# Two query blocks of the forgetting heads share a bank, a mask product and a place of transposes

## The reference

```python
def block(args):
    i, qd, qf, cq = args
    ...
    sf = jnp.einsum('bqhd,bkhd->bhqk', qf, fk).astype(jnp.float32) * (FOX_HEAD_DIM ** -0.5)
    sf = sf + jnp.transpose(cq, (0, 2, 1))[..., :, None] - cum_k[..., None, :]
    pf = jax.nn.softmax(jnp.where(causal, sf, NEG), axis=-1)
    of = jnp.einsum('bhqk,bkhd->bqhd', pf.astype(fv.dtype), fv)
```

## Time and profile before

| | us |
|---|---|
| median of 3 runs | 1096.33 (1096.22 to 1096.59) |
| span of the profiled execution | 1095.5 |
| PE busy in it | 1082.5 |
| ACT busy | 569.1 |
| DVE busy | 539.3 |
| POOL busy | 433.3 |

### The profile page before, as it was taken

How to read it: one execution, slowest core, us unless ns; L and a number is a source line. 1 busy time by engine, 2 the same in 40 slices (tenths; PEclk the granted TensorE clock), 3 DMA queues, 4 the chain that set the end, 5 groups by cost and what they waited for, 6 DMA issues and landing times.

```text
span 1095.5 us, 14926 instructions
## 1 busy us (share of the span) xinstructions
PE 1082.5 (99%) x5685; PEld 888.8 (81%) x5685; DVE 539.3 (49%) x1155; ACT 569.1 (52%) x1086; POOL 433.3 (40%) x236
## 2 busy tenths in 40 slices
PE   8999999999999999999999999999999999999998
PEld 7878878778887788888778787789888888888886
DVE  3739789788765224142445455535111115544444
ACT  6556767777678642353565565555222224333333
POOL 4234342342433344553143322344444445444441
PEclk9999999999999999999999999999999999999999
DMA  8133121221322332623222321222333333322312
GB/s 254 52 97 87 40 77 40 78 59 39 97 59 58 96 96 96 230 78 81 78 70 66 97 78 58 77 80 79 112 96 96 96 97 127 104 97 96 97 58 77
DMA packets 140530, 97.24 MB, mean 89 GB/s; under 512 B 9014, under 2 KB 125091, under 8 KB 140459
## 3 DMA queue, kind: packets, MB, share of 16 engines
q1 hardware_dynamic: 138728, 95.03, 29.4%
q10 hardware_dynamic: 1730, 1.25, 0.4%
HBM read 94.14 MB, written 2.91 MB: 89 GB/s over the span
## 4 chain that ended last, share of the span: by engine, by line
PE 95%; ACT 2%; DVE 1%; DMA 1%; issue 0%; POOL 0%; SPq 0%; ACTq 0%; DVEq 0%
PE bank L467 32%; PE bank L1196 14%; PE bank L1214 14%; PE bank L508 4%; PE bank L893 4%; PE bank L867 4%; PE bank L877 4%; PE bank L1227 2%; PE bank L686 1%; PE bank L617 1%; PE bank L629 1%; PE bank L710 1%; PE bank L1042 1%; PE bank L1004 1%; PE bank L482 1%; PE bank L1024 1%
## 5 line engine op out<-in xcount | busy, mean ns | idle before, releaser
L2485 POOL TENSOR_TENSOR ring<-raw_ring,ring 128x1024 fp32r<-128x1024 f32 x160 | 386.8, 2421 | 569.3 <-ACT ring L1241 569.3
L467 PE MATMUL bank<-hT,ring 128*128 128x512 f32 x1536 | 394.9, 402 | 0.7 <-ACT rawsb L1316 0.5
L467 PEld LDWEIGHTS bank<-hT,ring 128*128 128x128 f32 x1536 | 277.9, 188 | 57.9 <-issue 6.5
L1241 ACT CAST ring<-raw_ring 128x1024 fp32r<-128x1024 f32 x160 | 167.3, 1047 | 109.6 <-PE bank L1214 88.8
L1196 PE MATMUL bank<-hT,ring 128*128 128x512 f32 x672 | 152.5, 389 | 0.0
L1214 PE MATMUL bank<-ring,ring_u 128*128 128x512 f32 x672 | 152.5, 389 | 0.0
L1214 PEld LDWEIGHTS bank<-ring,ring_u 128*128 128x128 f32 x672 | 126.2, 188 | 26.2
L1196 PEld LDWEIGHTS bank<-hT,ring 128*128 128x128 f32 x672 | 126.1, 188 | 26.1
L2460 DVE TENSOR_TENSOR ring_u<-u,ring_u 128x1024 fp32r<-128x1024 f32 x32 | 80.7, 2529 | 73.8 <-ACT ring_u L1821 73.8
L2465 DVE TENSOR_TENSOR u<-u 128x512 f32<-128x512 f32 x32 | 22.9, 714 | 138.8 <-ACT u L1828 138.8
L1828 ACT ACTIVATE u<-bank 128x512 f32<-128x512 f32 x32 | 19.1, 598 | 114.9 <-PE bank L1196 108.4
(11 more groups left out here) (296 smaller groups left out, 1493.3 us busy)
## 6 DMA issues: line engine op xcount, KB each, us to landing
raw_ring<-in_w_in SPq DMA_DIRECT2D x144, 256.0 KB, 3.3
raw_ring<-in_w_up SPq DMA_DIRECT2D x64, 256.0 KB, 3.2
raw_ring<-in_w_down SPq DMA_DIRECT2D x64, 256.0 KB, 2.8
raw_ring<-in_w_out SPq DMA_DIRECT2D x32, 256.0 KB, 2.9
x<-in_x SPq DMA_DIRECT2D x8, 512.0 KB, 5.4
raw_ring<-in_w_branch_sb SPq DMA_DIRECT2D x8, 256.0 KB, 2.7
raw_ring<-in_w_branch_gdn SPq DMA_DIRECT2D x8, 256.0 KB, 3.2
cum<-cums SPq DMA_DIRECT2D x4, 512.0 KB, 5.5
```

The source lines that it names most:

```text
L467: p = pe.matmul(bank, m.slab_k8(n % 4)[:, a, k, :], m.hT[:, b, k, :], start=term == 0, stop=term == 23)
L1241: act.copy(m.ring[:, q, 0, :], m.raw_ring[:, q, :]).then_inc(s.slab_hi[q], 1)
L2485: pool.tensor_tensor(m.ring[:, q, 1, :], m.raw_ring[:, q, :], m.ring[:, q, 0, :].bitcast(F32), ALU.subtract).then_inc(s.slab_lo[q], 1)
```

## The change

The blocks of a forgetting head are handled in three units instead of four steps: unit 0 holds blocks 0 and 1 (128 and 256 columns side by side in the bank), unit 1 is block 2, unit 2 is block 3. For unit 0 there are still two maxima, two exponentials, two scalings and two copies per head, but one negation, one reciprocal and one mask product of 256 columns. `fox_z(i, 0)` issues twelve score matmuls at the place where it issued six, the separate place of block 1 is gone, and the six transposes of unit 0 stand together behind `diff_rows_T(i, 0, 0)`. On DVE and ACT the orders are set anew to match; semaphore counts change with them. In the last group the later places move too: block 2's scores stand at `tiles.to(41)`, block 3's ahead of `diff_z(i, 0, 1, 1)`, and on ACT and DVE block 3's exponentials and maxima stand ahead of the last `diff_exp` and `diff_weights`.

```diff
+FOX_UNITS = ((0, 1), (2,), (3,))
+FOX_STEPS = (0, 6, 10, 14)
+FOX_ACT = (0, 4, 6, 8)
+def fox_parts(u):
+    at = 0
+    for n, t_ in enumerate(FOX_UNITS[u]):
+        yield n, t_, at, at + (t_ + 1) * P
+        at += (t_ + 1) * P
 # TensorE
+    def fox_z(i, u):
...
         for k, (a, b) in enumerate(PARTS):
+            for n, t_, low, high in fox_parts(u):
+                for h in range(2):
+                    hp = slice(64 * h, 64 * h + 64)
+                    pe.matmul(banks[6 + h][:, low:high], qf[hp, a, t_ * P:(t_ + 1) * P], kf[hp, b, 0:high - low],
+                              start=k == 0 and n == 0, stop=k == 2, skip_group_check=n > 0)
         for h in range(2):
+            if u == 0:
+                o = banks[6 + h].rearrange("p (n w) -> p n w", n=2)[:, :, 0:P]
+                mask = m.causal_b.unsqueeze(1).broadcast_to([P, 2, P])
...
+            pe.matmul(o, m.ident_b, mask, start=False, stop=True, skip_group_check=True).then_inc(s.f_ps[h], 1)
 # TensorE, early groups
         fox_z(i, 0)
-        tiles.to(31)
-        fox_rows_T(i, 0, 0)
-        tiles.to(34)
-        fox_rows_T(i, 1, 0)
         tiles.to(51)
         diff_rows_T(i, 1, 0, pairs)
         tiles.to(54)
         diff_rows_T(i, 0, 0, pairs)
-        fox_z(i, 1)
+        fox_rows_T(i, 0, 0)
+        fox_rows_T(i, 1, 0)
         tiles.to(58)
         diff_av(i, 1, 0, pairs)
         tiles.to(63)
         diff_av(i, 0, 0, pairs)
-        fox_rows_T(i, 1, 1)
-        fox_rows_T(i, 0, 1)
 # TensorE, last group
-    tiles.to(20)
+    tiles.to(28)
+    diff_rows_T(i, 0, 0, last_pairs)
     fox_rows_T(i, 1, 0)
     fox_rows_T(i, 0, 0)
-    tiles.to(25)
-    tiles.to(28)
-    diff_rows_T(i, 0, 0, last_pairs)
-    fox_z(i, 1)
     tiles.to(41)
     diff_rows_T(i, 1, 0, last_pairs)
-    fox_rows_T(i, 1, 1)
+    fox_z(i, 1)
     tiles.to(46)
-    fox_rows_T(i, 0, 1)
     diff_av(i, 1, 0, last_pairs)
-    tiles.to(47)
     tiles.to(48)
     diff_z(i, 1, 1, 0, last_pairs)
-    fox_z(i, 2)
     diff_z(i, 1, 1, 1, last_pairs)
     tiles.to(49)
     diff_av(i, 0, 0, last_pairs)
+    fox_rows_T(i, 0, 1)
+    fox_rows_T(i, 1, 1)
     tiles.to(53)
     diff_z(i, 0, 1, 0, last_pairs)
-    fox_rows_T(i, 0, 2)
-    fox_rows_T(i, 1, 2)
+    fox_z(i, 2)
     diff_z(i, 0, 1, 1, last_pairs)
     tiles.to(54)
     diff_rows_T(i, 1, 1, last_pairs)
     tiles.to(55)
-    fox_z(i, 3)
     diff_rows_T(i, 0, 1, last_pairs)
...
 # ScalarE, early groups
         tile_b(g)
         diff_exp(i, 1, 0, 0)
-        fox_p(i, 0, 0)
         diff_exp(i, 0, 0, 0)
         diff_exp(i, 1, 0, 1)
         diff_exp(i, 0, 0, 1)
-        fox_p(i, 1, 0)
         diff_p(i, 0, 0, 2)
         diff_p(i, 1, 0, 4)
-        fox_exp(i, 0, 1)
-        fox_exp(i, 1, 1)
+        fox_p(i, 0, 0)
+        fox_p(i, 1, 0)
         tile_b(g + 1)
...
 # ScalarE, last group
     split(SLABS_OUT2 + 5)
-    fox_exp(i, 0, 2)
-    fox_exp(i, 1, 2)
+    fox_p(i, 0, 1)
+    fox_p(i, 1, 1)
     diff_square(i, 0, 0)
     diff_exp(i, 1, 1, 0)
     diff_exp(i, 1, 1, 1)
-    fox_p(i, 0, 2)
-    fox_p(i, 1, 2)
+    fox_exp(i, 0, 2)
+    fox_exp(i, 1, 2)
     diff_exp(i, 0, 1, 0)
     diff_exp(i, 0, 1, 1)
     diff_p(i, 1, 1, 5)
     diff_p(i, 0, 1, 4)
-    fox_exp(i, 0, 3)
-    fox_exp(i, 1, 3)
...
 # VectorE, early groups
         fox_max(i, 0, 0)
         fox_max(i, 1, 0)
+        diff_max(i, 1, 0, 1, 5)
+        diff_max(i, 0, 0, 0, 2)
+        diff_max(i, 0, 0, 1, 3)
         fox_recip(i, 0, 0)
-        diff_max(i, 1, 0, 1, 5)
         fox_normed(i, 0, 0)
         fox_recip(i, 1, 0)
         fox_normed(i, 1, 0)
-        diff_max(i, 0, 0, 0, 2)
-        diff_max(i, 0, 0, 1, 3)
         diff_weights(i, 1, 0)
         diff_weights(i, 0, 0)
...
 # VectorE, last group, from diff_weights(i, 1, 0) on, as it is after the change
+    fox_max(i, 0, 1)
+    fox_max(i, 1, 1)
+    diff_o(i, 1, 0, 5)
+    fox_recip(i, 0, 1)
+    fox_recip(i, 1, 1)
+    fox_normed(i, 0, 1)
+    fox_normed(i, 1, 1)
+    diff_max(i, 1, 1, 0, 5)
+    diff_max(i, 1, 1, 1, 5)
+    diff_o(i, 0, 0, 4)
+    diff_max(i, 0, 1, 0, 4)
+    diff_weights(i, 1, 1)
+    fox_max(i, 0, 2)
+    fox_max(i, 1, 2)
+    diff_max(i, 0, 1, 1, 4)
+    diff_weights(i, 0, 1)
+    fox_recip(i, 0, 2)
+    fox_normed(i, 0, 2)
+    fox_recip(i, 1, 2)
+    fox_normed(i, 1, 2)
+    diff_o(i, 1, 1, 5)
+    diff_o(i, 0, 1, 4)
```

More of the change, by code:

```diff
@@ L1700, in diff_mix, with fox_exp, fox_p @@
         act.copy(m.mix[:, 0, i, :], banks[bank]).then_inc(s.d_mhi, 1)
[L1702 to L1712, removed]
+    def fox_exp(i, h, u):
+        st = m.stat[:, 32 + 6 * h:38 + 6 * h]
+        act.wait_ge(s.f_dve[h], 14 * i + FOX_STEPS[u] + len(FOX_UNITS[u]) + 1)
+        for n, _, low, high in fox_parts(u):
+            sc = fox_rows[h][:, low:high]
+            act.activation(sc, sc, ACT.Exp, bias=st[:, n:n + 1], accum_out=st[:, 2 + n:3 + n]).then_inc(s.f_act[h], 1)
+    def fox_p(i, h, u):
+        act.wait_ge(s.f_ps[h], 7 * i + 2 * u + 2)
+        for _, t_, low, high in fox_parts(u):
+            dst = m.fox_wT[:, 3 - t_, 4 - t_:5, :] if h else m.fox_wT[:, t_, 0:t_ + 1, :]
+            act.copy(dst.rearrange("p c f -> p (c f)"), banks[6 + h][:, low:high]).then_inc(s.f_act[h], 1)
     def fox_mix(i):
-        act.wait_ge(s.f_ps[0], 9 * (i + 1))
-        act.wait_ge(s.f_ps[1], 9 * (i + 1))
+        act.wait_ge(s.f_ps[0], 7 * (i + 1))
+        act.wait_ge(s.f_ps[1], 7 * (i + 1))
         act.copy(m.mix[:, 0, 4 + i, :], banks[6]).then_inc(s.f_mhi, 1)
@@ L1778, in scalar_program @@
     split(SLABS_OUT2 + 2)
-    fox_exp(i, 1, 1)
[L1780 to L1785, removed]
+    diff_p(i, 0, 0, 4)
+    fox_p(i, 1, 0)
+    fox_p(i, 0, 0)
+    split(SLABS_OUT2 + 3)
+    diff_p(i, 1, 0, 5)
+    fox_exp(i, 0, 1)
+    fox_exp(i, 1, 1)
     diff_square(i, 1, 0)
     split(SLABS_OUT2 + 5)
-    fox_exp(i, 0, 2)
-    fox_exp(i, 1, 2)
+    fox_p(i, 0, 1)
+    fox_p(i, 1, 1)
     diff_square(i, 0, 0)
@@ L1798, in scalar_program @@
     diff_p(i, 0, 1, 4)
-    fox_exp(i, 0, 3)
-    fox_exp(i, 1, 3)
     diff_square(i, 1, 1)
     diff_square(i, 0, 1)
-    fox_p(i, 0, 3)
-    fox_p(i, 1, 3)
+    fox_p(i, 0, 2)
+    fox_p(i, 1, 2)
     fox_mix(i)
@@ L2346, in fox_recip, with fox_max @@
[L2346 to L2354, removed]
+    def fox_max(i, h, u):
+        st, count = stat[:, 32 + 6 * h:38 + 6 * h], len(FOX_UNITS[u])
+        dve.wait_ge(s.f_ps[h], 7 * i + 2 * u + 1)
+        if u == 0:
+            dve.wait_ge(s.f_c[i % 2], 16 * (i // 2 + 1))
+        for n, _, low, high in fox_parts(u):
+            dve.tensor_tensor_reduce(out=fox_rows[h][:, low:high], in0=banks[6 + h][:, low:high], in1=m.cum[:, 2 * (i % 2) + h, 0:high - low], scale=1.0,
+                                     scalar=-3.0e38, op0=ALU.add, op1=ALU.max, accum_out=st[:, n:n + 1]).then_inc(s.f_dve[h], 1)
+        dve.wait_ge(s.f_dve[h], 14 * i + FOX_STEPS[u] + count)
+        dve.tensor_scalar(st[:, 0:count], st[:, 0:count], -1.0, None, ALU.mult).then_inc(s.f_dve[h], 1)
@@ new lines, in fox_recip, with fox_normed @@
+    def fox_recip(i, h, u):
+        st, count = stat[:, 32 + 6 * h:38 + 6 * h], len(FOX_UNITS[u])
+        dve.wait_ge(s.f_act[h], 8 * i + FOX_ACT[u] + count)
+        dve.reciprocal(st[:, 4:4 + count], st[:, 2:2 + count]).then_inc(s.f_dve[h], 1)
+    def fox_normed(i, h, u):
+        st, count = stat[:, 32 + 6 * h:38 + 6 * h], len(FOX_UNITS[u])
+        dve.wait_ge(s.f_dve[h], 14 * i + FOX_STEPS[u] + count + 2)
+        for n, _, low, high in fox_parts(u):
+            sc = fox_rows[h][:, low:high]
+            dve.tensor_scalar(sc, sc, st[:, 4 + n:5 + n], None, ALU.mult).then_inc(s.f_dve[h], 1)
```

123 lines of the change are left out of this document (41 added, 82 removed).

## The result

Median after: 1106.38 us (1106.29 to 1106.53), against 1096.46 (1096.22 to 1097.15) for the kernel before in the same session: 9.9 us slower, a ratio of 1.0092 (95% interval 1.008 to 1.0104). The forecast was slower by 5.7; its range ended at 1103.6. The profiled execution spans 1105.0 us, 9.5 more than before.

A forecast was written before the change was run, and what follows sets the result against it. PE taken as the bound, its issued work plus its waits: 1095.5 + 1.1 (early groups) + 3.4 (last group) + 1.2 (clock) = 1101.2 us span; median 0.8 above, 1102.0; range 1095.9 to 1103.6.

The forecast's parts named there:

- What bounds the kernel: Whole kernel: time is what PE issues plus each wait of PE; PE busy 1082.5 of 1095.5 us.
- PE's list: Each of four groups: separate place saves 0.83 us, unit 0 adds 0.40; net -0.43, in all -1.7.
- Early groups, ACT's chain: Early groups: ACT's chain ends 1.57 us later; PE waits 0.27 and 0.5 at two transpose sets; net +0.37 each.
- Early groups, DVE: Early groups: DVE adds 0.41 us by a second maximum ahead of ACT's chain; POOL's order is untouched.
- Last group, waits: Last group: new PE waits of 1.0, 0.7 and 3.7 us (third at last diff_rows_T); fox_av +3.4 by the walk.
- The clock: Last group: the 3.7 us wait halves the granted clock for 3.4 us, costing 1.2.
- The sum: Whole span: 1095.5 + 1.1 + 3.4 + 1.2 = 1101.2 us; median 0.8 above, 1102.0.
- The clock didn't stay up: Rival, last group: the clock stays up through the third wait, 1100.8 us; chance 0.22.
- the third wait was not short: Rival, last group: block 3's maxima hide ahead of diff_weights(1,1), about 3 of 3.7 us disappear, 1097.8; chance 0.15.
- ACT and DVE were not fast enough: Rival: ACT's and DVE's chains grow too little for any new wait on PE, 1093.9 us; chance 0.12.
- the other side: Faster outcome, if no new wait arises: PE's list counts, -1.7 us, giving 1093.2 to 1094.6; chance 0.12.
- wait on a slab's low part: Sign of being wrong: PE waits for POOL's low part at stream matmul 48, margin put at only 0.3 us.

The follow-up runs named there:

- x1_other_form: Kernel after, with unit 0's scalings on DVE in the tensor_scalar form that also writes an accumulator; nothing moved: 1103.77 us.
- x7_early_reordered: Kernel after, early groups with differential maxima and exponentials first, scalings behind diff_weights, slab cast earlier; last group as before the change: 1095.30 us against 1096.32 before.
- x3_weights_first: Kernel after, with unit 0's reciprocals and scalings behind both diff_weights on DVE in the early groups: 1104.89 us.
- x5_last_weights: Kernel after, last group's final diff_max, diff_weights and two diff_exp moved ahead of block 3's maxima and exponentials: 1103.44 us.
- x4_busy_wait: Kernel after, with nine useless 512-column matmuls filling PE's third wait of the last group: 1105.05 us.
- x6_all_reordered: x7_early_reordered's early order, plus the changed last group with forgetting and differential steps interleaved: 1099.18 us against 1096.32 before.
- x9_no_hold: x6_all_reordered with the last group's second unit-1 scaling ahead of diff_max(1,1,0) and both unit-1 scalings in accumulator form: 1095.86 us against 1096.65 before.
- x2_early_only: Kernel after, with the last group's PE, ACT and DVE programs as before the change: 1100.50 us.

## Why the prediction was wrong in size

By its own steps:

- **What bounds the kernel: right.** PE's list plus its waits accounts for the whole difference. By the group times: 3 x 1.48 + 3.64 + 2.11 = 10.2 us; what stands ahead of the first group was 0.7 shorter in the profile after, within the spread from execution to execution, which gives the 9.5 of the spans.
- **PE's list: right.** From the first differential score to the stream's return the place at unit 0 grew from 1.80 to 2.26 us (+0.46, predicted +0.40), the separate place went, and with all waits gone the group is 0.41 shorter (predicted 0.43), so the separate place and the rest of the list gave up 0.87 (predicted 0.83). The Trainium skill's figure for a sustained stream of 128-column matmuls (TensorE: Matmul & The Clock Gate, section Back-to-back issue gap), which had given an estimated 0.24, doesn't fit heads that run in pairs.
- **Early groups, ACT's chain: right.** It ended at 591.78, and with the hold gone (x1_other_form) PE waits 0.31 and 0.44 at the two sets of transposes, counted as start to start against x7_early_reordered, where 0.27 and 0.5 were forecast.
- **Early groups, DVE: the step that failed.** The prediction let ACT's chain alone set the end of `diff_weights`. Its sum has no term for the new scalings on DVE, which at their duration in the trace of before (0.28 us for 128x128) would have fitted beside that chain, and it put POOL's order down as untouched. POOL's order is indeed untouched; but the change brings four such scalings, ahead of `diff_weights`, into the time in which POOL takes tile 2's low part. The first one lasted 2.25. The first wait was 1.3 (start to start) instead of 0.27, so each of three groups took 1.48 - 0.37 = 1.1 us more than forecast: 3.3 of the 4.4 us by which the median was missed, where the range had allowed 0.3 a group. x1_other_form shows it by the form, x3_weights_first by the place. The trace of before could have told; all engines around the last group's `fox_normed` of block 1 in the kernel before:

```profile
685.79 2.40 POOL L2485 TENSOR_TENSOR ring<-raw_ring,ring 128x1024 fp32r<-128x1024 f32 x1 [12.63 <-ACT ring L1241]
...
687.69 0.92 DVE L2354 TENSOR_SCALAR b<-b,stat 128x256 f32<-128x256 f32 x2
```

  The first of these two parts took 0.66 instead of 0.34 and ended at 688.35, 0.16 after POOL's instruction. The Trainium skill (SBUF — State Buffer, section Who interferes with whom) has a rule for this: GpSimd and VectorE share a pair of ports as an exclusive lock, the one that issues first keeps it for its whole instruction, and a VectorE `tensor_scalar` can want it unless it is the form that also writes its accumulator. The traces agree where POOL came first: the end 0.08 us after POOL's in the kernel after and 0.16 in that of before, and no hold for the accumulator form; that a port is the cause no run shows by itself. I had read the durations and not looked at what ran beside them.
- **Last group, waits: right.** 0.89, 0.66 and 3.51 us idle against 1.0, 0.7 and 3.7; waits and list together 3.64 against 3.4. That the third is the queue behind block 3's maxima and exponentials is shown by x5_last_weights.
- **The clock: right in kind, short by 0.9.** It fell, as in the earlier trace rows, but stayed low for 6.83 us instead of 3.4; by x4_busy_wait that cost 2.1 instead of 1.2. The 3.4 was taken from one fall near the start of the span. In x1_other_form, with the same order in the last group, the low stretch was 3.4 us (705.9 to 709.3) and cost 1.4, close to the forecast; in x3_weights_first 6.83 us cost 2.7. In all three the fall began inside the wait, 1.4 to 3.1 us after its start. Why it lasts 3.4 in one and 6.8 in two the runs don't say.
- **The sum.** 1102.0 + 3.3 (hold) + 0.2 (last group) + 0.9 (clock) = 1106.4. The group times alone give 10.2 us where the medians differ by 9.9; such a difference is within what the stage ahead of the first group varies by, up to 1.0 us.
- **The rivals.** The clock didn't stay up; the third wait was not short; ACT and DVE were not fast enough in the order given. In the early groups of x7_early_reordered they are, and only then does the other side appear, by 1.0 us. No wait on a slab's low part arose in the groups: the danger from that low part was on DVE, not on PE.

## What to carry to other kernels

When an edit moves or adds a VectorE instruction, look at what GpSimd does at its new time, not only at its duration at its old one: here 0.28 us became 2.25 behind the start of a 2.4 us subtraction, and either the accumulator form or another place made it 0.35 or less again. Gathering short steps into fewer, larger ones takes only their fixed costs off the bounding engine (0.4 us a group); the helpers' chains grow by more, so let the products that come first go through the helper engines first. Price a wait on TensorE of some microseconds with its clock (1.4 to 2.7 us here for one and the same wait of 3.51), and treat the length of the low stretch as uncertain by several times (3.4 to 13.65 us in these profiles).

## What the hardware showed that I had not expected

- Even a `tensor_scalar` of 128x2 elements was held for 1.96 us beside POOL, while the reciprocal of the same 128x2 shape (0.16 us at 588.80 in the kernel after, 0.04 after POOL's start) wasn't.
- The plain `tensor_scalar` isn't the only form that is held. The last step of `diff_weights`, which reads two tensors, was held too where it began 0.14 us after POOL. In x6_all_reordered (DVE, POOL):

```profile
684.93 2.67 DVE L2318 SCALAR_TENSOR_TENSOR b<-b,stat,b 128x384 f32<-128x384 f32 x1
...
684.79 7.40 POOL L2473 TENSOR_TENSOR ring<-raw_ring,ring 128x1024 fp32r<-128x1024 f32 x3 [12.78 <-ACT ring L1247]
```

  It takes 0.62 elsewhere. In x9_no_hold it took 2.70 (685.09 to 687.79); PE's transposes of its result began at 687.84, without idle time, so it cost nothing there, but nothing was to spare either.
- A wait of 1.92 us was followed by 13.65 us at half clock though PE was then busy for 3.2 to 3.4 of each 3.4 us; a wait of 3.51 us was followed by 6.83 in two kernels and by 3.4 in a third, and waits of 1.2 us (x4_busy_wait, x5_last_weights) by none. The Trainium skill (TensorE: Matmul & The Clock Gate, section Why this matters for your kernels) warns of long idle gaps; here one of under 2 us was enough in one kernel, and not in each of its executions. The low stretch near the start of the span is missing in the profiles of x2_early_only, x3_weights_first and x5_last_weights. Neither when the clock falls nor for how long is explained by these runs.
